# Moving every sixth batch's first one-hots to GpSimd, with another order of first loads, fillings and last items

## The chip, the core and the metric

The kernel runs on one core of a Trainium2 chip. Its engines each follow their own instruction list: TensorE (PE), VectorE (DVE), ScalarE (ACT), GpSimd (POOL) and SyncE (SP, which here only issues transfers). They wait for one another by semaphores. The metric is the device time of one launch in microseconds. Inputs and weights lie in HBM and all arithmetic is in float32, except for some one-hots in bf16.

## The reference, cut to what matters

One decoder layer over 1024 tokens of width 1024, with 16 learned tokens ahead of them. The first half mixes tokens: one projection to four groups of channels with pooling windows and to three gates of a short convolution, norms, and an output projection. The second half picks experts by product keys and sums them:

```python
def peer_retrieve(xn, w_query, sub_keys):
    T = xn.shape[0]
    q = (xn @ w_query).reshape(T, N_PEER_HEADS, 2, D_QUERY_HALF)
    s = jnp.einsum('thpc,hpkc->thpk', q.astype(jnp.float32), sub_keys.astype(jnp.float32))
    s1, i1 = lax.top_k(s[:, :, 0], PEER_TOPK)
    s2, i2 = lax.top_k(s[:, :, 1], PEER_TOPK)
...
    top_s, pos = lax.top_k(cand_s, PEER_TOPK)
    idx = jnp.take_along_axis(cand_i, pos, axis=-1)
    gates = jax.nn.softmax(top_s, axis=-1)
    return idx, gates
...
    def block(args):
        xblk, iblk, gblk = args
        u = expert_u[iblk]
        v = expert_v[iblk]
        act = jax.nn.gelu(jnp.einsum('tkd,td->tk', u, xblk).astype(jnp.float32), approximate=False)
        return jnp.einsum('tk,tkd->td', (gblk * act).astype(v.dtype), v)
```

Here cand_s are the 256 sums of the two halves' best 16, and cand_i their expert ids (i1 * 128 + i2). There are 8 heads, 16384 experts and 16 picked per head, so 128 per token.

The result is added to the residual and normed once more.

## The kernel before

Tokens come in eight tiles of 128, two to a pass, so there are four passes, n = 0 to 3. For four of the tiles the experts are gathered row by row ("rows", 128 experts of u and 128 of v per tile: 1024 rows of 512 KB each, one expert for each of the 128 tokens). For the other four tiles ("dense") all 16384 experts are multiplied with TensorE, and a table of gates, mostly zeros, picks the ones that count.

**The passes (to about 661 us).** TensorE walks through a list `steps`: bcv and pa (input projection), pool, outp, ynorm, outp, turn (transposes), query and score. Four pairs of psum banks are used in turn, so that step s waits until step s - 4 has been emptied, by ACT or by DVE. DVE does the pooling, the convolution and the norms, and between them, at named places, `fill(n, where)`: a planner (`take`) puts units there until their assumed costs (`COST`) reach the number in `FILL`. The units rank the experts of the two tiles of the pass before: four `keys`, `cands`, two `pairs`, `digits`, `pick`, `keep` for each tile, in this order, with the second tile's first keys between the first tile's digits and pick. When nothing is left to rank, a place is filled with rows (`gathered_row`, L1175, 1.35 each by the planner). `pick` needs 16 activations of ACT (`pick_places`, L859, line 864 in the profile), which ACT does right after a step that the planner finds from the costs (`step_at`, `picks_after`). Rows sit in a ring of eight slots: GpSimd issues row r when row r - 8 has been used (L677 to L680).

**The scatter.** The first dense tile's gates are scattered to the table in HBM with 128 indirect transfers of GpSimd, 16 per head (`scatter`, L643). `head_after` (L641) puts heads 0 to 2 behind the issue of row `rows_by[1] + 7` and heads 3 to 7 behind row `rows_by[2] + 7`, where `rows_by[n]` is the number of rows used up to the end of pass n. A head waits for the transfers of the heads before it.

**The gate tables (662 to 821 us).** Three dense tiles' gates become tables by 48 batches of eight tokens. A batch needs two sets of eight one-hots (128x128 each) in one of three buffers. The gated ones are DVE's in all batches (L1467). The first ones are DVE's in even batches (one instruction, L1463) and ACT's in odd ones (eight Square, then one Relu: `first_hots`, L980 to L987, begun one odd batch ahead). TensorE multiplies them (L798), ACT copies the two banks out of psum (L1009), and SyncE stores a chunk each four batches. A buffer comes free when TensorE has done the batch three before. In batches 5, 13, 21, 29, 37 and 45 TensorE also does a score tile of the dense part (L785).

**The dense part (to 2547 us).** TensorE takes tiles of scores (L785, 16 instructions, 6.87 us) and pieces of output sums (L831, the same), eight and eight in groups. ACT makes the gelu (L993), DVE multiplies with the gates (`gate`, L1252) and adds the pieces (`sum`, L1258). Four psum banks hold pieces: piece i waits until sum i - 4 is done. DVE's list is one `order`: the ranking of the last two tiles and all rows that are left (`late`), with gates and sums put between them by their share of the cost, times `DENSE_SPEED`. With a value of 1.0 the last sum comes with the last row. Then follow `total`, `finish` and `dense_out`, and the stores.

**First loads.** SyncE issues the first half of x, the second half, the small vectors, two weight blocks (1 MB each), x of pass 1 and the rest (L521 to L529). ACT squares each half (L876), DVE scales it with g_mix (L1395), TensorE starts with `pa` 0 (L717), one weight block and eight blocks of x.

## Time and profile before

| | us |
|---|---|
| median of 3 runs | 2557.34 |
| lowest, highest | 2557.06, 2560.21 |
| the profiled execution | 2559.86 |
| its span | 2558.1 |

| engine | busy us | share | instructions |
|---|---|---|---|
| PE | 2474.3 | 97% | 7561 |
| DVE | 1971.3 | 77% | 4252 |
| ACT | 424.1 | 17% | 782 |
| POOL | 1452.8 | 57% | 1169 |

The mean granted clock of TensorE is 0.991 of full. The transfers move 857.68 MB, 335 GB/s over the span. The profile is of the profiled execution; its times count from the start of the span. A row of a timeline shows the start, the time taken, the engine, the line of the code, the operation with what it writes and reads, and in brackets how long the engine was idle before it and what ended that. Busy shares are averages over stages with different limits, so each stage is read by itself.

### The profile page before, as it was taken

What the parts mean: (1) busy time and instruction counts of PE and PEld (TensorE: products, weight loads), DVE (VectorE), ACT (ScalarE), POOL (GpSimd) and SP (SyncE); (2) the same over time, 40 slices, a digit from 0 to 9 for tenths busy, and PEclk for the clock granted to TensorE, in tenths of its full rate; (3) what the DMA queues carried; (4) which work ended last, traced back from release to release, by engine and by line L of the source; (5) the groups of instructions that cost most, each with busy time, mean ns of one, the idle gap of its engine ahead of it and who ended that gap; (6) DMA issues with size and microseconds to landing.
All of it is one profiled execution on the core that took longest, in us unless ns stands there. A gap on an engine that the chain in (4) does not pass through costs nothing.

```text
span 2558.1 us, 24120 instructions
## 1 busy us (share of the span) xinstructions
PE 2474.3 (97%) x7561; PEld 1360.4 (53%) x7561; DVE 1971.3 (77%) x4252; ACT 424.1 (17%) x782; POOL 1452.8 (57%) x1169
## 2 busy tenths in 40 slices
PE   8999998998888899999999999999999999999998
PEld 7687785867766344444444444444444444444443
DVE  4308879778779788777898778779787877888877
ACT  0213213221887000110010100000000000000001
POOL 0000487677601267666665767667676776766664
PEclk9999999998999999999999999999999999999999
DMA  8544886865666899989999999999999999999997
GB/s 336 214 156 163 315 300 167 347 188 132 198 190 201 333 356 374 396 318 385 388 413 391 383 385 414 394 418 419 419 386 397 412 394 420 419 407 403 420 401 262
DMA packets 288079, 857.68 MB, mean 335 GB/s; under 512 B 42064, under 2 KB 99408, under 8 KB 273360
## 3 DMA queue, kind: packets, MB, share of 16 engines
q0 software_dynamic: 167184, 541.73, 55.4%
q1 hardware_dynamic: 108416, 289.25, 30.0%
q10 hardware_dynamic: 12352, 25.17, 2.6%
q8 instruction: 60, 0.98, 0.1%
q14 instruction: 67, 0.55, 0.1%
HBM read 807.75 MB, written 48.30 MB: 335 GB/s over the span
## 4 chain that ended last, share of the span: by engine, by line
PE 85%; DVE 6%; ACT 4%; DMA 1%; issue 1%; DVEq 1%; POOL 1%; SPq 1%; ACTq 0%
PE pairs L831 34%; PE pairs L785 33%; PE pairs L699 12%; ACT arena L985 2%; PE pairs L742 1%; PE pairs L717 1%; PE pairs L798 1%; ACT arena L1009 1%; DMA arena<-gate_tables 1%; PE pairs L769 1%; ACT pick_all L864 1%; POOL ring L679 1%; DVE topi L1073 0%; DVE topi L1065 0%; ACT arena L987 0%
## 5 line engine op out<-in xcount | busy, mean ns | idle before, releaser
L679 POOL DMA_INDIRECT ring<-in_expert_u,idx x512 | 660.7, 1290 | 610.7 <-DVE dots L1186 343.5
L831 PE MATMUL pairs<-arena 128*128 128x512 f32 x2048 | 883.4, 593 | 7.0 <-DVE arena L1252 6.3
L785 PE MATMUL pairs<-arena 128*128 128x512 f32 x2048 | 882.5, 592 | 0.0
L679 POOL DMA_INDIRECT ring<-in_expert_v,idx x512 | 574.7, 1122 | 290.2 <-DVE arena L1197 129.9
L1186 DVE CUSTOM_DVE_ANT_0 junk<-ring,xf 128x1024 bf16<-128x1024 f32 x512 | 610.5, 1223 | 157.1 <-DMA ring<-in_expert_u,idx 153.0
L831 PEld LDWEIGHTS pairs<-arena 128*128 128x128 f32 x2048 | 389.6, 190 | 498.4 <-issue 497.5
L785 PEld LDWEIGHTS pairs<-arena 128*128 128x128 f32 x2048 | 388.6, 190 | 486.5 <-issue 486.5
L1197 DVE SCALAR_TENSOR_TENSOR arena<-ring,arena 128x1024 f32<-128x1024 f32 x381 | 471.7, 1284 | 63.8 <-DMA ring<-in_expert_v,idx 62.5
L699 PE MATMUL pairs<-arena 128*128 128x256 f32 (+1 forms) x1792 | 399.7, 386 | 7.2 <-ACT arena L946 4.2
L699 PEld LDWEIGHTS pairs<-arena 128*128 128x128 f32 x1792 | 345.5, 193 | 59.5 <-ACT arena L946 5.1
L993 ACT ACTIVATE arena<-pairs 128x512 f32<-128x512 f32 x128 | 76.4, 597 | 1176.2 <-PE pairs L785 1176.2
L650 POOL DMA_INDIRECT gate_tables<-gate,place x128 | 210.8, 1647 | 57.9 <-issue 38.8
L1197 DVE SCALAR_TENSOR_TENSOR xf<-ring,arena,xf 128x1024 f32<-128x1024 f32 x126 | 154.4, 1282 | 8.8 <-DMA ring<-in_expert_v,idx 8.8
L1252 DVE TENSOR_TENSOR arena<-arena 128x512 f32<-128x512 f32 x128 | 87.6, 688 | 61.2 <-ACT arena L993 48.9
L1258 DVE TENSOR_TENSOR arena<-arena,pairs 128x512 f32<-128x512 f32 x128 | 87.5, 684 | 51.6 <-PE pairs L831 50.9
L1467 DVE TENSOR_SCALAR arena<-iota,arena 128x128 f32<-128x128 f32 x384 | 101.3, 347 | 25.5 <-PE pairs L798 25.5
L742 PE MATMUL pairs<-arena 128*128 128x512 f32 x256 | 114.2, 603 | 5.3 <-DVE arena L1377 5.3
L798 PE MATMUL pairs<-arena 128*128 128x128 f32 x768 | 91.4, 277 | 28.1 <-ACT arena L1009 25.3
L798 PEld LDWEIGHTS pairs<-arena 128*128 128x128 f32 x768 | 88.2, 192 | 34.0 <-issue 30.9
L864 ACT ACTIVATE pick_all<-digit,place 128x256 bf16<-128x256 f32 x128 | 80.4, 723 | 42.0 <-DVE digit L1130 41.7
L742 PEld LDWEIGHTS pairs<-arena 128*128 128x128 f32 x256 | 49.4, 194 | 65.3 <-issue 55.8
L1062 DVE MAX8 tops<-arena 128x8 f32<-128x128 f32 x112 | 24.4, 280 | 61.9 <-ACT arena L961 60.7
(174 smaller groups left out, 1062.1 us busy)
## 6 DMA issues: line engine op xcount, KB each, us to landing
arena<-in_w_all SPq DMA_DIRECT2D x80, 1024.0 KB, 6.1
arena<-in_uT SPq DMA_DIRECT2D x128, 512.0 KB, 6.7
arena<-in_expert_v SPq DMA_DIRECT2D x128, 512.0 KB, 8.8
arena<-gate_tables SPq DMA_DIRECT2D x32, 1024.0 KB, 11.3
gate_tables<-arena SPq DMA_DIRECT2D x11, 2048.0 KB, 9.0
gate_tables<-junk ACTq DMA_DIRECT2D x4, 2048.0 KB, 14.0
ring<-in_expert_u,idx POOLq DMA_INDIRECT x512, 8.9
ring<-in_expert_v,idx POOLq DMA_INDIRECT x512, 8.3
```

The lines of the kernel that those rows point to most:

```text
L650: nc.gpsimd.indirect_dma_start(out=g_flat, out_offset=bass.IndirectOffsetOnAxis(ap=place[:, k:k + 1], axis=0), in_=gate[:, k:k + 1], in_of ...
L679: nc.gpsimd.indirect_dma_start(out=ring[:, r % RING, :], out_offset=None, in_=expert_u if table == "u" else expert_v, in_offset=bass.Indir ...
L699: last = nc.tensor.matmul(out_, w[:, k, c * P:(c + 1) * P], xn[:, k, :], start=(k == 0), stop=(k == KD - 1))
L742: last = nc.tensor.matmul(pair[:, q * 512:(q + 1) * 512], yT[:, NG * (1 - half) + k, t * P:(t + 1) * P], w_out[q].rearrange("p k n -> p (k ...
L785: last = nc.tensor.matmul(score_bank[x], uslot[:, x % USLOTS, k * P:(k + 1) * P], xfT[:, k, :], start=(k == 0), stop=(k == KD - 1))
L798: last = nc.tensor.matmul(g_bank[(2 * b + m) % 4][:, q * KEYS:(q + 1) * KEYS], hots[:, c, 0, 4 * m + q, :], hots[:, c, 1, 4 * m + q, :], s ...
L831: last = nc.tensor.matmul(o_bank[n % 4], gated[:, x % GSLOTS, t * P:(t + 1) * P], vrows[:, j, half * 512:(half + 1) * 512], start=(j == 0) ...
L864: last = nc.scalar.activation(pick_hot[:, a], digit[:].rearrange("p h s k -> p k (h s)"), ACT.Square, scale=32.0, bias=place16[:, a:a + 1])
L1186: nc.vector.tensor_tensor_reduce(out=junk[:, r % 2, :], in0=row, in1=xf[:, t % 2, :], scale=1.0, scalar=0.0, op0=ALU.mult, op1=ALU.add, ac ...
L1197: nc.vector.scalar_tensor_tensor(out=to[:, k % 2, :], in0=row, scalar=weight[:, k:k + 1], in1=h2 if k == 0 else to[:, k % 2, :], op0=ALU.m ...
L1252: nc.vector.tensor_tensor(s, s, gtab[a // GJ % 2][:, :, a % GJ, :], ALU.mult).then_inc(w_ready, 1)
L1467: last = nc.vector.tensor_scalar(hots[:, c, 1, t, :], iota[:], routeT[:, 1, k:k + 1], routeT[:, 2, k:k + 1], ALU.is_equal, ALU.mult)
```

## The change

Batches with b % 6 = 5 (5, 11, ..., 47) get their first one-hots from GpSimd instead of ACT: eight `tensor_scalar` with is_equal per batch, behind the point at which GpSimd has issued row `rows + RING - 1`, where `rows` is the number of rows used ahead of the tables. The semaphore of the first one-hots is split in two. The smalls are loaded first, and a weight block is issued after each half of x. The numbers of `FILL` for outp, query, y and y2 get smaller, and `DENSE_SPEED` becomes 0.99.

```diff
@@ -76,9 +76,9 @@
 FILL = [[(f"conv{g}", 4.0) for g in range(4)] + [("gate", gate), ("y", y), ("y2", y2), ("outp", outp), ("query", query)]
-        for gate, y, y2, outp, query in ((0.0, 0.0, 0.0, 0.0, 0.0), (4.0, 13.0, 6.0, 10.0, 70.0), (4.0, 13.0, 6.0, 10.0, 70.0), (0.0, 10.0, 3.0, 0.0, 66.0))]
+        for gate, y, y2, outp, query in ((0.0, 0.0, 0.0, 0.0, 0.0), (4.0, 13.0, 6.0, 2.0, 66.0), (4.0, 13.0, 6.0, 2.0, 66.0), (0.0, 8.0, 0.0, 0.0, 66.0))]
 HOT_FILL = 0.0
-DENSE_SPEED = 1.0
+DENSE_SPEED = 0.99
 FIRST_FILL = 42.0
 KEYS_ROWS = 3
@@ -295,7 +295,8 @@
         d_gates = sem("d_gates")
         turned = sem("turned")
         turned_out = sem("turned_out")
-        hot_first = sem("hot_first")
+        hot_act = sem("hot_act")
+        hot_pool = sem("hot_pool")
         hot_gated = sem("hot_gated")
         table_full = sem("table_full")
         table_out = sem("table_out")
@@ -496,6 +497,11 @@
             elif kind == "sum" and a == GROUPS - 1 and b % 2 == 1:
                 beside[x].append(("dense_root", b // 2))
+
+
+        BY_POOL = [b for b in range(BATCHES) if b % 6 == 5]
+        BY_ACT = [b for b in range(BATCHES) if b % 2 == 1 and b % 6 != 5]
+
         block = ctx.enter_context(nc.Block())
         @block.sync
@@ -518,11 +524,11 @@
                     sp.wait_ge(pe_step if by == "step" else w_freed, count)
                 sp.dma_start(wslot[k % WSLOTS].rearrange("p k n -> p (k n)"), w_all[uses[k][0], :, :]).then_inc(w_loaded[k % WSLOTS], 16)
+
+            sp.dma_start(smalls[:], small).then_inc(small_in, 16)
             for s in range(2):
                 sp.dma_start(xnT[0][:, s * NG:(s + 1) * NG, :], hT[:, s * NG:(s + 1) * NG, BASE[0]:BASE[0] + COLS]).then_inc(x_first[s], 16)
-            sp.dma_start(smalls[:], small).then_inc(small_in, 16)
-            load_w()
-            load_w()
+                load_w()
             load_x(1)
             sp.dma_start(poolw.rearrange("p g n -> p (g n)"), pool_w).then_inc(const_in, 16)
             sp.dma_start(skT, sub_keys).then_inc(const_in, 16)
@@ -657,6 +663,16 @@
                     pool.wait_ge(rows_used, first_row["u", t - 2] + HK)
                 pool.dma_start(xf[:, t % 2, :], of_tile(xf_d, GATHERED_TILE[t])).then_inc(xf_in[t % 2], 16)
+            def first_hots(b):
+                c = b % HOTBUFS
+                pool.wait_ge(table_full, 2 * (b - HOTBUFS) + 2)
+                if b // (P // HOTS) > 0:
+                    pool.wait_ge(turned_out, b // (P // HOTS))
+                for t in range(HOTS):
+                    k = b * HOTS + t
+                    last = nc.gpsimd.tensor_scalar(hots[:, c, 0, t, :], iota[:], routeT[:, 0, k:k + 1], None, ALU.is_equal)
+                last.then_inc(hot_pool, 1)
+
             for i, (table, t) in enumerate(ROWS):
                 if table == "u":
                     load_xf(t)
@@ -674,6 +690,10 @@
                     pool.dma_start(h2, of_tile(h2_d, GATHERED_TILE[t])).then_inc(h2_in, 16)
                 for k in range(HK):
                     r = HK * i + k
+                    if r == rows + RING:
+
+                        for b in BY_POOL:
+                            first_hots(b)
                     if r >= RING:
                         pool.wait_ge(rows_used, r - RING + 1)
                     nc.gpsimd.indirect_dma_start(out=ring[:, r % RING, :], out_offset=None, in_=expert_u if table == "u" else expert_v,
@@ -789,8 +809,10 @@
             for b in range(BATCHES):
                 c = b % HOTBUFS
                 pe.wait_ge(hot_gated, b + 1)
-                if b % 2 == 1:
-                    pe.wait_ge(hot_first, b // 2 + 1)
+                if b in BY_ACT:
+                    pe.wait_ge(hot_act, BY_ACT.index(b) + 1)
+                elif b in BY_POOL:
+                    pe.wait_ge(hot_pool, BY_POOL.index(b) + 1)
                 for m in range(2):
                     if 2 * b + m >= 4:
                         pe.wait_ge(table_out, 2 * b + m - 3)
@@ -984,7 +1006,7 @@
                 for t in range(HOTS):
                     nc.scalar.activation(hots[:, c, 0, t, :], iota[:], ACT.Square, scale=-1.0, bias=routeT[:, 0, b * HOTS + t:b * HOTS + t + 1])
                 act.drain()
-                nc.scalar.activation(hots[:, c, 0], hots[:, c, 0], ACT.Relu, scale=-4.0, bias=ones[:, 0:1]).then_inc(hot_first, 1)
+                nc.scalar.activation(hots[:, c, 0], hots[:, c, 0], ACT.Relu, scale=-4.0, bias=ones[:, 0:1]).then_inc(hot_act, 1)
             def gelu_tile(x):
                 if x >= GSLOTS:
@@ -998,7 +1020,7 @@
             for b in range(BATCHES):
                 if b - 1 in AFTER_BATCH:
                     gelu_tile(AFTER_BATCH.index(b - 1))
-                if b % 2 == 1 and b + 2 < BATCHES:
+                if b % 2 == 1 and b + 2 in BY_ACT:
                     first_hots(b + 2)
                 for m in range(2):
                     n = 2 * b + m
```

With the new numbers the planner puts into the places (units of the tile ranks, with the rows used):

| place | before | after |
|---|---|---|
| pass 1, outp | pick 0, keep 0, keys 1 (third) | pick 0 |
| pass 1, query | from the fourth keys of 1; rows 0 to 27 | keep 0, third and fourth keys of 1, ...; rows 0 to 18 |
| pass 2, outp | pick 2, keep 2, keys 3 (third) | pick 2 |
| pass 2, query | ...; rows 28 to 56 | keep 2, third keys of 3, ...; rows 19 to 39 |
| pass 3, y2 | digits 4 | nothing |
| pass 3, query | keys 5, ...; rows 57 to 63 | digits 4, keys 5, ...; rows 40 to 46 |
| ACT's picks for ranks 1 and 3 | after query step 0 | after query step 1 |
| ACT's picks for rank 4 | after the second outp | after the second turn |

In the dense part the order has gate 127 behind row 991 before and behind row 1001 after the change. Its last items were sum 4, rows 1012 to 1015, sum 5, dense_out 1, rows 1016 to 1019, sum 6, rows 1020 to 1023, sum 7, dense_out 2, dense_out 3, total 3, finish 3; they become sum 4, rows 1022 and 1023, total 3, sum 5, dense_out 1, sum 6, sum 7, dense_out 2, dense_out 3, finish 3.

## Rows read from the trace of the kernel before

**Rows 1.** The chain that ended last, by time: start us, us, what.

```profile
817.47 3.59 PE pairs L798 x32
```

**Rows 2.** The page's 40 slices: what the transfers moved.

```profile
GB/s 336 214 156 163 315 300 167 347 188 132 198 190 201 333 356 374 396 318 385 388 413 391 383 385 414 394 418 419 419 386 397 412 394 420 419 407 403 420 401 262
```

**Rows 3.** Timeline of the start: start us, us, engine, line, operation [idle before].

```profile
6.28 1.11 ACT L876 ACTIVATE arena<-arena 128x1088 f32<-128x1088 f32 x1 [0.42 <-DMA arena<-in_hT]
...
9.04 5.62 PE L717 MATMUL pairs<-arena 128*128 128x272 f32 x16 [9.04 <-DMA arena<-in_w_all]
```

**Rows 4.** Timeline of TensorE, passes 1 to 3.

```profile
271.40 3.44 PE L748 MATMUL pairs<-ident,arena 128*128 128x128 f32 x16 [2.23 <-DVE arena L1387]
...
437.30 1.07 PE L748 MATMUL pairs<-ident,arena 128*128 128x128 f32 x8 [3.24 <-DVE arena L1387]
...
565.44 7.03 PE L742 MATMUL pairs<-arena 128*128 128x512 f32 x16
...
577.53 9.61 PE L742 MATMUL pairs<-arena 128*128 128x512 f32 x16 [5.07 <-DVE arena L1377]
```

**Rows 5.** Query stretches: busy us (instructions) by engine, granted clock, DMA share, GB/s.

```profile
118.00:175.00 57.00, 55.49 (x256) 48.56 (x256) 1.64 (x4) 4.45 (x5) 0.72 (x1) 1.00 0.46 161
276.00:335.00 59.00, 58.54 (x256) 50.69 (x256) 48.96 (x155) 15.07 (x22) 31.35 (x19) 0.95 0.89 330
441.00:499.00 58.00, 57.45 (x256) 50.13 (x256) 46.25 (x149) 13.68 (x20) 38.73 (x26) 0.96 0.84 311
```

**Rows 6.** Timeline of GpSimd: scatters of heads, then row loads.

```profile
513.00 1.62 POOL L650 DMA_INDIRECT gate_tables<-gate,place  x1 [0.30 <-issue]
...
679.12 1.56 POOL L650 DMA_INDIRECT gate_tables<-gate,place  x1 [0.30 <-issue]
...
688.56 0.94 POOL L679 DMA_INDIRECT ring<-in_expert_u,idx  x1 [0.30 <-issue]
```

**Rows 7.** Timeline of DVE: a pick, and where two fillings end.

```profile
304.19 2.29 DVE L1136 TENSOR_TENSOR pick_all<-topf,pick_all 128x4096 bf16<-128x4096 bf16 x1 [3.65 <-ACT pick_all L864]
...
345.57 0.44 DVE L1302 TENSOR_TENSOR arena<-arena 128x271 f32<-128x271 f32 x1
...
510.40 0.44 DVE L1302 TENSOR_TENSOR arena<-arena 128x271 f32<-128x271 f32 x1
```

**Rows 8.** Timeline of GpSimd: a select, row loads beside DVE and alone.

```profile
1.15 0.29 POOL L631 TENSOR_SCALAR_AFFINE_SELECT ident<-ident 128x128 f32<-128x128 f32 x1 [0.63 <-DVE ident L1048]
...
299.37 1.99 POOL L679 DMA_INDIRECT ring<-in_expert_u,idx  x1 [0.30 <-issue]
301.66 0.94 POOL L679 DMA_INDIRECT ring<-in_expert_u,idx  x1 [0.30 <-issue]
```

**Rows 9.** Timeline of the table stage: batch 5, a plain pair.

```profile
676.35 2.02 PE L798 MATMUL pairs<-arena 128*128 128x128 f32 x16 [1.01 <-ACT arena L1009]
...
693.02 2.44 ACT L985 ACTIVATE arena<-iota,arena 128x128 f32<-128x128 f32 x8
...
694.35 1.22 DVE L1463 TENSOR_TENSOR arena<-iota,arena 128x1024 f32<-128x1024 f32 x1
...
695.49 4.20 DVE L1467 TENSOR_SCALAR arena<-iota,arena 128x128 f32<-128x128 f32 x16
...
698.50 2.44 ACT L985 ACTIVATE arena<-iota,arena 128x128 f32<-128x128 f32 x8
```

**Rows 10.** DVE by line, 2000 to 2200: busy us, mean ns, idle before.

```profile
L1186 DVE CUSTOM_DVE_ANT_0 junk<-ring,xf 128x1024 bf16<-128x1024 f32 x66 | 79.1, 1224 | 23.9 <-DMA ring<-in_expert_u,idx 23.6
L1197 DVE SCALAR_TENSOR_TENSOR arena<-ring,arena 128x1024 f32<-128x1024 f32 x51 | 63.7, 1285 | 15.2 <-DMA ring<-in_expert_v,idx 14.8 <-issue 0.2
```

**Rows 11.** Waits of DVE, 816 to 2547: us in total, times, longest.

```profile
DVE arena L1258 <- PE pairs L831: 50.9, 42, 1.6
DVE arena L1252 <- ACT arena L993: 48.9, 30, 3.6
```

**Rows 12.** Timeline of the end.

```profile
2550.74 1.22 DVE L1238 TENSOR_TENSOR xf<-xf 128x1024 f32<-128x1024 f32 x1
```

## Prediction

> **What bounds the kernel now.** I read the page first (busy shares, the 40 slices, the granted clock), then the chain of work in order of time, the stretches between its changes of character, and for each stretch what its leading engine waited for. The reader should see three parts. Up to about 661 us the projections run in four passes (n = 0 to 3). From 662 to 821 us come the gate tables, 48 batches of one-hots, whose last TensorE work starts at 817.47 [rows 1]. After a loading gap of some 38 us the dense part runs from 859 us on without a break to 2547 us. In the dense part only order and supply matter: TensorE's tiles and pieces of 6.87 us each follow one another, and the change takes none of them away. So time can be won ahead of 821 us and behind 2547 us, and lost anywhere.
>
> The sum is made against the profiled execution: 2559.86 us, of which the span is 2558.1. It is 2.5 us above the median of the runs, 2557.34, and I take differences from it over to the median.
>
> **First loads.** TensorE starts at 9.04, held by the first weight block, which is queued behind both halves of x and the small vectors [rows 3]. In the new order one half of x (544 KB) is no longer ahead of it: at the 336 GB/s of the page's first slice [rows 2] that is 1.6 us. The second half of x now lands about when the weights do today, just ahead of 9.04 (I take 8.8) instead of 6.2; its square takes 1.1 us [rows 3] and the first scaling 0.3, which make it ready at 10.2. TensorE, started at 7.4, reaches its fifth block (0.70 us each, 5.62 for eight) at 10.2. So there is hardly a second wait, and I take 1.3 us (0 to 2).
>
> **Fillings.** The planner's lists can be followed. In passes 1 and 2 "outp" keeps only pick; keep and one keys unit go to the head of "query", and the rows there fall from 28 to 19 and from 29 to 21. In pass 3 digits leaves "y2" for "query". So 47 rows instead of 64 are used before the tables, and 17 more remain. Removed from TensorE's path:
> - pass 1: idle 2.23 ahead of the turns, which then took 3.44 at a lowered clock [rows 4], and a query stretch of 58.54 us of matmuls at a mean granted clock of 0.95 of full, where pass 0 took 55.49 at 1.00 [rows 5]. The clock had fallen to its lower level (1.2 of 2.4 GHz) after the idle time. With DVE's add_half some 6.5 us earlier the turns don't wait: 2.2 + 3.0 and about 0.8 of the turns, 6.0.
> - pass 2: 3.24 idle ahead of the turns [rows 4] and 0.4 between them, 57.45 against 55.49 in the query [rows 5], some 1.3 of slow turns: 7.0. A short wait at ynorm stays, because DVE gains about as much as TensorE.
> - pass 3: 5.07 idle and an output product of 9.61 instead of 7.03 [rows 4]: 7.7. ACT's pick for rank 4, 10 us long, stood between two outp steps and kept the y root waiting; it moves behind the turns.
>
> Together with the start the tables could begin 22.0 us earlier.
>
> **What GpSimd does meanwhile.** Here the two halves of the change meet. first_hots for batch 5 stands in GpSimd's order behind five heads of scatter and seven row loads. Today the scatters start at 513.00, the last one at 679.12, and the seventh row load ends at 689.5 [rows 6]: 176.5 us of issue work that nothing here shortens. They start when DVE has used the last row of pass 2's filling, 510.4 [rows 7]. How much earlier is that? In pass 1 the picks on ACT now follow the second query step, not the first: they end at 311.8 (TensorE's query begins at 272.9 and a step takes 13.9; ACT needs 11.1 behind the second) instead of 304.2 [rows 7], and the 9 rows fewer behind them are worth 15.6 at 1.73 us a row, the 34 us of 311.5 to 345.6 over 20 rows, so DVE leaves the pass 8 us earlier than 345.6 [rows 7]. In pass 2 the same placing ends the picks 2 us later than today and there are 8 rows fewer (13.9): 11.9 earlier. With the start that is 13.2. GpSimd thus comes to batch 5 at 689.5 - 13.2 = 676.3. One set is eight operations on 128x128. No row shows this operation on GpSimd. Nearest below is its select on 128x128, 0.29 us; nearest above its indirect issue, 0.94 us alone and up to 1.99 beside DVE's row work [rows 8]. I take 0.35, as the select has the same shape, so 3 us a set (2.3 to 8). TensorE could have begun batch 5 at 676.35 - 22.0 = 654.3 [rows 9] and begins it at 679.3. It waits 25 us there, so that batch 5 begins 3 us later than today: all that the start and the fillings won, and 3 us more, is paid back in this one wait.
>
> **The tables.** From batch 5 to the end takes 144.7 us today (676.35 to 821.06) [rows 1, 9]. An odd batch's first one-hots and four copies make ACT's pair of batches 5.48 long (693.02 to 698.50) [rows 9]. DVE's pair is 1.14 + 4.20 = 5.3 [rows 9], TensorE's 3.6 [rows 1], and once in eight batches a score tile adds 6.87. Taking a third of the sets from ACT therefore uncovers DVE at once, 0.2 us lower in a plain pair; more of the gain lies in the pair with the score tile. TensorE alone would need 43 x 1.8 + 6 x 6.87 = 119 and DVE alone 43 x 2.67 = 115; I take 138, nearer to today's 144.7 because DVE's 5.3 follows ACT's 5.48 so closely (range 126 to 150). The tables end at 679.3 + 138 = 817.3, 3.7 us earlier than today.
>
> A set on GpSimd reads and writes SBUF beside DVE. The issue of a row load took 1.99 us while DVE worked on rows with two inputs and 0.94 while it waited [rows 8], so the two do hold each other up in some pairings. The Trainium skill ("SBUF — State Buffer", section "SBUF: two separate sides") says that GpSimd and a DVE instruction of two SBUF inputs, or of a two-port mode, exclude each other for whole instructions. If it holds for the one-hots, the tables end at 834 instead of 817; no row here shows the two side by side, and the case is a rival below.
>
> **The dense part.** It has DENSE_SPEED 0.99 and 17 rows more. Counted in the two orders, 928 rows stand ahead of gate 127 today, 955 after the change: 27 more. Between 2000 and 2200 us DVE waited for rows alone and used 66 + 51 of them, 1.71 us a row with the items between [rows 10], so 27 rows cost 46 us. DVE's idle time for TensorE and ACT in 816 to 2547 is 50.9 + 48.9 = 99.8 us [rows 11]; this is the cover, and about 54 are left of it. It isn't even: at 2000 to 2200 there is none, and psum lets a sum be three pieces (20 us) late, a last gate of a group only the two tiles behind it, and gate 127 nothing. I take 4 us of TensorE waiting at the last group (0 to 20).
>
> **The end.** Today total 3 starts at 2550.74, behind the dense outputs, then come root and finish [rows 12]. In the new order total and root lie ahead of the last three sums, and after dense_out 3 only finish is left: the 1.2 of total and 1.6 of waiting for the root fall away, 2.9 us (2 to 3).
>
> Sum: -3.7 + 4 - 2.9 = -2.6, so 2557.34 - 2.6 = 2554.7 us.
>
> **Rivals.**
> 1. GpSimd comes earlier. If the rows of the passes land faster than 1.7 us each or the picks on ACT aren't late, DVE's end of pass 2 follows TensorE's 20 us instead of 13, and with a table pace of 130 the sum is -2.6 - 7 - 7 = 2541. For it: DVE's waits in both passes are for rows alone. Against it: the picks follow TensorE's steps. Chance 0.27.
> 2. Slower, by the supply of rows in the dense part. The 54 us of cover are an average, and where DVE is bound by rows the new order asks for 2.6% more of them a step. If rows come at 1.71 us throughout, also near the end, gate 127 is late by 10 to 20 us, as each row too few ahead of it costs 1.7 us. This decides from the point where 27 more rows use up the cover between 2200 and 2490. For it: no cover at all in 2000 to 2200 [rows 10]. Against it: much of the 99.8 lies behind 2200. Time 2554.7 - 4 + 17 = 2568. Chance 0.20.
> 3. DVE and GpSimd exclude each other in the tables. Seven sets of 2.4 us taken from DVE, which is then the bound, are 17 us, and the tables end at 834 instead of 817: 2571. For it: 1.99 beside 0.94 [rows 8]. Against it: a set is short beside six batches. The Trainium skill's sentence above would give this result. Chance 0.10.
> 4. The change doesn't do what it says: ACT's sets weren't the pace, and the passes gain nothing since another wait follows each that goes. Then only start and end are left, 2553 to 2558. Chance 0.05.
>
> The forecast has 0.38. It lies between 2549 and 2561.
>
> **How the numbers follow.** A measurement of this kernel can tell about 0.2% from no change, 5 us. Faster by more than that (under 2552.2): all of rival 1, 0.09 of the forecast: 0.36. Slower (over 2562.5): rivals 2 and 3, less a little of 2: 0.29. The rest is 0.35. The range takes in rivals 1 and 2 and reaches to the price of 3: 2538 to 2573. The forecast's own range is 2549 to 2561.
>
> **What would show it.** In the profile after: the first TensorE matmul near 7.4; no idle ahead of the turns in passes 1 and 2; the query stretches of these passes at a clock of 1.00; the first batch of the tables near 640; a wait of TensorE of some 25 us ahead of batch 5, released by GpSimd; the first GpSimd set near 676 and eight operations of about 0.35 us; the end of the tables near 817; DVE's idle time for TensorE and ACT near 50 us; a wait of a few us at the last group's first piece; 8 us between the last matmul and the end instead of 11. The prediction is wrong if GpSimd reaches batch 5 before TensorE does, if its operations take over 0.7 us each (a set must fit in two batches), or if DVE's cover in the dense part goes to nothing.

## The result

The changed kernel is slower: 2575.7 us, median of five runs (2567.2 to 2578.0), beside 2560.1 for five runs of the kernel before. The ratio is 1.0052, with a 95% interval of 1.0038 to 1.0066. In ten later runs it was 1.0020 (1.0000 to 1.0041), beside a kernel before that ran in 2555 to 2578. The two medians stand for a loss of some 5 to 13 us, and the two intervals together reach from nothing to 17. The forecast was 2554.7 with a range up to 2573; the median of 2575.7 lies above that range.

The profiled execution took 2578.0 us, with a span of 2576.2, against 2558.1 before: 18.1 longer. The table sets the steps of the sum beside each other. The "waits" of TensorE in the dense part are summed here from the starts of successive instructions of tiles and pieces: what lies between two starts beyond the 0.43 us of one, wherever that is over 0.12 us. They hold the idle time and the slower instructions at a lowered clock behind it. "Early" are those within 25 us of the first piece.

| profiled execution, us | before | after, predicted | after, measured |
|---|---|---|---|
| first TensorE matmul | 9.04 | 7.4 | 8.82 |
| tables begin | 662.0 | 640 | 644.0 |
| batch 5 begins | 676.3 | 679.3 | 678.1 |
| tables end | 821.0 | 817.3 | 819.3 |
| waits around the first pieces | 9.0 | 9 | 12.3 |
| waits in the rest of the dense part | 0 | 4 | 18.7 |
| last matmul ends | 2546.8 | 2547 | 2567.8 |
| from there to the end of the span | 11.3 | 8 | 8.3 |

So the first third ended close to where the sum had it: what the passes won went into one wait at batch 5. The 18 us come from behind 821 us: -1.8 from the tables, +3.3 and +18.7 of waits, +0.8 of single instructions behind them that start 0.1 us or less too late, and -3.0 at the end.

**The profile after, beside the rows of before.** Timeline of TensorE, to be held against [rows 3] and [rows 4] (start us, us, engine, line, operation, idle before it and what ended it; the lines of the code stand some 20 further on in the changed kernel):

```profile
8.82 5.35 PE L737 MATMUL pairs<-arena 128*128 128x272 f32 x16 [8.82 <-DMA arena<-in_w_all]
...
269.03 1.91 PE L768 MATMUL pairs<-ident,arena 128*128 128x128 f32 x16
...
347.45 8.84 PE L719 MATMUL pairs<-arena 128*128 128x256 f32 x27 [4.25 <-DMA arena<-in_w_all]
...
429.56 1.91 PE L768 MATMUL pairs<-ident,arena 128*128 128x128 f32 x16
...
573.57 1.06 PE L768 MATMUL pairs<-ident,arena 128*128 128x128 f32 x8 [3.79 <-DVE arena L1409]
...
655.34 1.95 PE L820 MATMUL pairs<-arena 128*128 128x128 f32 x16
678.07 3.75 PE L820 MATMUL pairs<-arena 128*128 128x128 f32 x16 [20.78 <-issue]
681.62 8.30 PE L805 MATMUL pairs<-arena 128*128 128x512 f32 x16
```

The turns of passes 1 and 2 no longer wait, and take 1.91 us, where those of pass 1 took 3.44. Two waits are left in the passes, and both stood there before:

```profile
351.96 8.22 PE L699 MATMUL pairs<-arena 128*128 128x256 f32 x37 [1.92 <-DMA arena<-in_w_all]
...
591.78 1.06 PE L748 MATMUL pairs<-ident,arena 128*128 128x128 f32 x8 [3.77 <-DVE arena L1387]
...
678.21 7.03 PE L785 MATMUL pairs<-arena 128*128 128x512 f32 x16
```

The wait for a weight block grew from 1.92 to 4.25 us, as TensorE comes to it earlier; the one for DVE between the turns of pass 3 stayed (3.77, now 3.79). At 678.07 is the wait at batch 5. Its end is put down to "issue"; the timeline of GpSimd shows who it was:

```profile
501.85 1.61 POOL L656 DMA_INDIRECT gate_tables<-gate,place  x1 [0.30 <-issue]
...
672.32 0.94 POOL L699 DMA_INDIRECT ring<-in_expert_u,idx  x1 [0.31 <-issue]
673.30 4.67 POOL L673 TENSOR_SCALAR arena<-iota,arena 128x128 f32<-128x128 f32 x8
695.37 6.23 POOL L673 TENSOR_SCALAR arena<-iota,arena 128x128 f32<-128x128 f32 x8 [17.40 <-PE pairs L820]
```

The scatters start at 501.85 instead of 513.00 [rows 6], GpSimd gets through them and seven row loads, makes the first set in 4.67 us, and TensorE starts the moment it ends. The windows show what else the wait costs (columns as in [rows 5]):

```profile
273.00:331.00 58.00, 56.80 (x273) 49.94 (x272) 44.45 (x162) 15.56 (x22) 24.11 (x18) 1.00 0.84 323
...
433.00:489.00 56.00, 55.49 (x256) 48.56 (x256) 42.84 (x161) 13.31 (x21) 19.86 (x14) 1.00 0.84 298
```

```profile
678.00:682.00 4.00, 3.93 (x17) 3.92 (x18) 0.14 (x1) 0.73 (x2) 0.00 (x0) 0.50 0.01 5
682.00:690.00 8.00, 8.00 (x19) 3.39 (x18) 3.14 (x9) 1.79 (x3) 0.00 (x0) 0.86 0.00 0
```

The query stretches of passes 1 and 2 now run at a granted clock of 1.00, where [rows 5] had 0.95 and 0.96. Behind the long wait the granted clock is 0.50, the lower of the two levels: batch 5 and the tile behind it take 3.75 + 8.30 us, against 2.02 [rows 9] + 7.03 before. So the long wait costs another 3 us behind it.

And the waits of TensorE from 862 us on. Before, this view has no line at all:

```profile
PE pairs L853 <- DVE arena L1274: 10.9, 6, 4.3
PE pairs L853 <- DVE arena L1280: 2.9, 3, 1.6
```

These are pieces of output that wait for DVE's gates (L1274) and sums (L1280). The view counts 13.8 us of idle time, and that is all there is. The starts give 18.7, as they also hold what the lowered clock costs behind a wait: behind the 4.32 us of idle time at 2516.86 the next matmuls start 0.85 us apart instead of 0.43 (granted clock 0.56 from 2517 to 2521), and behind the 2.59 at 1198.17 as well (0.63 from 1200 to 1204), some 2 us each. The other seven waits, of 1.6 us or less, have no such matmuls behind them. The early waits of 12.3 us are 9.1 of idle time and 3.2 of this. DVE's own rows tell why the gates are late, in the waits of 816 to 2560 us; the lines for PE and ACT belong against [rows 11]:

```profile
DVE junk L1208 <- DMA ring<-in_expert_u,idx: 165.6, 156, 4.3
DVE arena L1219 <- DMA ring<-in_expert_v,idx: 94.6, 99, 2.1
DVE xf L1219 <- DMA ring<-in_expert_v,idx: 24.6, 29, 2.3
...
DVE arena L1280 <- PE pairs L853: 6.5, 5, 2.5
...
DVE arena L1274 <- ACT arena L1015: 2.8, 3, 2.3
```

DVE now waits 285 us for rows (205 before) and 9 us for TensorE and ACT (99.8 before). The 27 rows more used up 90 of the 100 us of cover, not the 46 that the prediction gave them. Yet DVE gets through no more rows: 116 between 2000 and 2200 us by the two lines of [rows 10], where the kernel before had 117. The chain of work that ended last shows such a case (start us, us, what): a row that is under way for 10.7 us, rows and a gate of DVE back to back behind it, and then the gate that the piece at 2516.86 had waited 4.3 us for.

```profile
2498.65 10.72 DMA ring<-in_expert_v,idx
...
2511.22 1.33 DVE xf L1219 x2
...
2516.03 0.69 DVE arena L1274
2516.72 0.14 issue
2516.86 51.00 PE pairs L853 x114
```

### The profile page after: what moved, and what is told of

Its sections match the earlier page's. It is cut to its first block, busy times and chain, and to the rows that moved or that the text cites. A ratio compares the mean times of both kernels' runs of the same rounds, so it can differ in the third digit from the quotient of the medians.

```text
span 2576.2 us, 24110 instructions
## 1 busy us (share of the span) xinstructions
PE 2476.7 (96%) x7561; PEld 1361.5 (53%) x7561; DVE 1976.7 (77%) x4252; ACT 399.8 (16%) x710; POOL 1495.8 (58%) x1233
## 4 chain that ended last, share of the span: by engine, by line
PE 50%; DMA 19%; POOL 14%; issue 8%; DVE 5%; ACT 2%; SPq 1%; DVEq 0%; ACTq 0%
PE pairs L719 15%; POOL ring L699 14%; PE pairs L853 14%; DMA ring<-in_expert_u,idx 11%; PE pairs L805 10%; DMA ring<-in_expert_v,idx 6%; PE pairs L762 4%; PE pairs L820 2%; PE pairs L737 2%; DVE junk L1208 1%; DVE arena L1219 1%; DMA arena<-gate_tables 1%; PE pairs L789 1%; DVE arena L1489 1%; DMA arena<-in_w_all 1%
## 5 line engine op out<-in xcount | busy, mean ns | idle before, releaser
L699 POOL DMA_INDIRECT ring<-in_expert_u,idx x512 | 649.6, 1269 | 517.3 <-DVE dots L1208 246.8
L699 POOL DMA_INDIRECT ring<-in_expert_v,idx x512 | 588.0, 1148 | 258.2 <-issue 121.6
L1489 DVE TENSOR_SCALAR arena<-iota,arena 128x128 f32<-128x128 f32 x384 | 105.3, 353 | 18.3 <-PE pairs L820 18.3
L1280 DVE TENSOR_TENSOR arena<-arena,pairs 128x512 f32<-128x512 f32 x128 | 87.0, 680 | 17.9 <-PE pairs L853 17.5
L673 POOL TENSOR_SCALAR arena<-iota,arena 128x128 f32<-128x128 f32 x64 | 45.2, 724 | 92.8 <-PE pairs L820 92.7
L1274 DVE TENSOR_TENSOR arena<-arena 128x512 f32<-128x512 f32 x128 | 87.2, 685 | 14.8 <-DMA arena<-gate_tables 11.3
```

Of the source, the lines that this page charges most:

```text
L699: nc.gpsimd.indirect_dma_start(out=ring[:, r % RING, :], out_offset=None, in_=expert_u if table == "u" else expert_v, in_offset=bass.Indir ...
L1274: nc.vector.tensor_tensor(s, s, gtab[a // GJ % 2][:, :, a % GJ, :], ALU.mult).then_inc(w_ready, 1)
L1280: nc.vector.tensor_tensor(piece, piece, o_bank[b % 4], ALU.add).then_inc(o_added, 1)
L1489: last = nc.vector.tensor_scalar(hots[:, c, 1, t, :], iota[:], routeT[:, 1, k:k + 1], routeT[:, 2, k:k + 1], ALU.is_equal, ALU.mult)
```

## The experiments

The first four take the change apart and the next two take parts back; the others ask who limits the rows, and whether the two prices found can be paid in another way. Each ratio is to the kernel before on the same chip, with its 95% interval. Where it says "one run", there is a profile and a single time. The waits are those of one profiled execution each; for the changed kernel, for speed 1.0 in it and for the fillings alone that is the slowest of their runs, so that their waits may be a few us over the usual.

### One part at a time

**The dense order alone.** In the kernel before:

```diff
-DENSE_SPEED = 1.0
+DENSE_SPEED = 0.99
```

> The kernel before with DENSE_SPEED 0.99 alone. Theory 1 (supply): TensorE stalls in the dense part when the rows that must be used ahead of a gate or a sum come too slowly, and what counts is the sum of the 17 rows more and the 1% more. Here only about 10 more rows stand ahead of gate 127, 17 us of DVE's 100 us of idle time: 0 to 4 us of stalls in the dense part, and an end 2.7 us shorter, so -3 to +2 us against before. Theory 2 (the order of the last items costs it by itself, because DVE is late for gate 127): a stall of 5 to 9 us at the last group already here, and +3 to +7 us.

Measured: 2560.9 us, ratio 0.9995 (0.9978 to 1.0011). Dense waits 0.1 us, early ones 10.1; the end takes 8.3 us instead of 11.3. Ten more rows ahead of gate 127 cost TensorE nothing, and the gain at the end is there but too small to be told in the median.

**The fillings alone.** In the kernel before, the changed `FILL` and nothing else.

> The kernel before with the changed fillings alone: 47 rows ahead of the tables instead of 64. The tables begin 18 us earlier, as in the changed kernel, and nothing waits for GpSimd, so they end some 17 us earlier. Theory 1 (supply): 17 more rows are 29 us of supply, which the 100 us of idle time of DVE cover nearly: 0 to 6 us of stalls; in sum -17 to -9 us against before. Theory 3 (each row put behind the tables costs TensorE time, as the dense part was at the limit of supply already): 17 x 1.3 = 22 us of stalls, in sum about +5.

Measured: 2551.5 us, ratio 0.9947 (0.9930 to 0.9965). The tables begin at 642.2 and, with no wait at batch 5, end at 803.9: 17.2 us earlier than before. But dense waits of 12.1 us and early ones of 10.8 (9.0 before) appear, and in this execution, of 2556.9 us, the last matmul comes only 2.9 earlier; in the ratio 13.6 us are left. Seventeen rows more behind the tables are enough to make TensorE wait.

**GpSimd's one-hots alone.** In the kernel before, `BY_POOL`, `BY_ACT`, the two semaphores and `first_hots` of GpSimd.

> The kernel before with the one-hots on GpSimd alone (b % 6 = 5), loads, fillings and speed as before. GpSimd ends its row loads at 689.5 as before and its first set takes 4.7 us beside nothing, so batch 5 begins at 694.2 instead of 676.35: 18 us of wait. The other 43 batches took 141 us in the changed kernel against 144.7. Theory 1: the tables end 14 us later and the dense part is as before: +12 to +16 us. Rival: the wait is absorbed by a faster table stage, 0 to +5.

Measured: 2573.7 us, ratio 1.0028 (1.0009 to 1.0047). Batch 5 begins at 693.5 instead of 676.3, held by GpSimd's set, and the tables end 11.3 us later, at 832.3; the last matmul follows 12.9 later. This part alone is a loss. TensorE and GpSimd meet there in the same way as in the changed kernel:

```profile
676.33 1.95 PE L821 MATMUL pairs<-arena 128*128 128x128 f32 x16
693.49 3.75 PE L821 MATMUL pairs<-arena 128*128 128x128 f32 x16 [15.21 <-issue]
```

**First loads alone.**

```diff
+            sp.dma_start(smalls[:], small).then_inc(small_in, 16)
             for s in range(2):
                 sp.dma_start(xnT[0][:, s * NG:(s + 1) * NG, :], ...)
-            sp.dma_start(smalls[:], small).then_inc(small_in, 16)
-            load_w()
-            load_w()
+                load_w()
```

> The changed order of first loads alone. The step of the prediction gave it 1.3 us. The changed kernel's profile showed a first matmul at 8.82 instead of 9.04 and nothing left of it in the first pass, so now: the first matmul near 8.8, the end of pass 0 and the start of the tables within 1 us of the kernel before, and the span within 0.2% of it.

Measured, one run: 2559.7 us, span 2557.9, the first matmul at 9.18, the tables from 662.0 to 821.0: no gain over the one profile of the kernel before. The first matmul varies from execution to execution, though. In the seven profiles with the old order of loads, of kernels that differ elsewhere, it starts at 9.04 to 9.91 (mean 9.60), in the seven with the new one at 8.33 to 9.18 (mean 8.90). So the step brings some 0.7 us at the first matmul; in the median of the runs this can't be seen. In the changed kernel the first half of x, alone in front now, is squared at 5.99 instead of 4.75 and the second at 10.04 instead of 6.28 [rows 3], while the weight block lands at 8.8. That fits transfers that share the bandwidth while they are under way, although they are issued one behind the other: with 544 KB less in front of it the weight block gains less than half of the 1.6 us of those bytes. That they share it is argued, not shown.

### The changed kernel with one part taken back

**Speed 1.0 in the changed kernel.**

```diff
-DENSE_SPEED = 0.99
+DENSE_SPEED = 1.0
```

> The changed kernel with DENSE_SPEED 1.0 again. Theory 1 (supply): 10 rows fewer ahead of gate 127, so the stalls of the dense part fall from 22 to 5 to 12 us and the end is 2.7 us longer again: -7 to -14 us against the changed kernel, about 2565 us. Theory 2 (the order of the last items): only the stall at the last group (7 us) goes. Theory 3 (17 rows): stalls stay at 18 to 22, and the time is that of the changed kernel or 2 us above it.

Measured: 2567.4 us, ratio 1.0009 (0.9991 to 1.0027). Dense waits fall from 18.7 to 9.2, and the end grows back to 11.3. The same ten rows that cost nothing in the kernel before cost 9.5 us here.

**Batch 5 back on ACT.** GpSimd makes the sets of 11, 17, ..., 47.

```diff
-        BY_POOL = [b for b in range(BATCHES) if b % 6 == 5]
-        BY_ACT = [b for b in range(BATCHES) if b % 2 == 1 and b % 6 != 5]
+        BY_POOL = [b for b in range(BATCHES) if b % 6 == 5 and b > 5]
+        BY_ACT = [b for b in range(BATCHES) if b % 2 == 1 and b not in BY_POOL]
```

> The changed kernel with batch 5's first one-hots on ACT again; GpSimd keeps batches 11, 17, ..., 47. Theory 1: GpSimd's order behind the scatters costs the tables 20.8 us at batch 5. Without it batch 5 runs at about 657 and batch 11, which begins at about 678 then, finds its set just in time (GpSimd comes free at 673). The tables end 14 to 20 us earlier, near 802; the dense part keeps its stalls of 20 us: 14 to 20 us under the changed kernel, 2556 to 2562. Rival: ACT, DVE and TensorE had used the wait to run ahead, so only 5 us come back.

Measured: 2555.6 us, ratio 0.9976 (0.9963 to 0.9989). Batch 5 begins at 660.0 and the tables end at 802.3, 17.0 earlier than in the changed kernel; dense waits stay, 17.3. From batch 5 to the end it is 142.3 us, where the fillings alone, without GpSimd, take 147.4. So the seven sets that are left do speed up the tables by some 5 us, but the set of batch 5 costs 17 through its wait, and the dense loss has nothing to do with the sets.

### Who limits the rows

Two theories were left for the late gates. Rows may be limited by what the transfers carry per us, or by latency: GpSimd's issue and eight slots of the ring.

**Ring of seven.** In the kernel before, `RING = 7`.

> The kernel before with a ring of 7 row slots instead of 8. If rows are limited by the latency of a slot's round trip (issue, landing, use, next issue), the supply becomes 7/8 as fast, a row takes 1.94 us instead of 1.7, and the dense part becomes 150 to 220 us longer. If it is limited by what the transfers move in all (397 GB/s in 900 to 2500 us), the ring is deep enough and the time grows by 0 to 25 us.

Measured, one run: 2576.9 us, span 2575.2, dense waits 14.4. A slot fewer costs some 16 us; a supply held by latency alone would lose an eighth of its pace, ten times as much. That it costs anything may be because the ring evens out the transfers' pace; this is argued, not shown.

**Rows of half the length.** The changed kernel, in which a row's load brings only 512 of the 1024 numbers (the other half of the ring stays zero; that part of the experts is left out of the computation), with as many transfers, issues and slots.

> The changed kernel with rows of half the length: each row transfer brings only the first 512 of 1024 numbers, the other half of each ring slot is zero from the start, so part of the computation is left out. DVE does the same work per row. If the limit is the number of bytes, DVE's waits for rows (285 us) fall to under 60 us and the stalls of TensorE in the dense part go to the 9 us at its beginning: about 2555 us. If it is the issue on GpSimd or the latency of the round trip, the waits stay above 180 us and so do the stalls.

Measured, one run: 2544.8 us, no dense wait, early ones 2.7. That is 10 us under what was expected, in good part because the early waits went too. The windows, first the changed kernel, then this one:

```profile
1500.00:2000.00 500.00, 499.01 (x1163) 220.55 (x1162) 397.34 (x531) 25.60 (x42) 351.89 (x291) 1.00 1.01 404
2000.00:2500.00 500.00, 495.88 (x1155) 219.01 (x1154) 414.28 (x459) 26.31 (x43) 356.44 (x304) 1.00 1.02 412
```

```profile
1500.00:2000.00 500.00, 500.00 (x1166) 221.35 (x1165) 405.00 (x550) 24.02 (x39) 386.34 (x303) 1.00 0.75 251
2000.00:2500.00 500.00, 500.00 (x1166) 221.35 (x1165) 411.61 (x436) 29.74 (x48) 364.91 (x305) 1.00 0.77 257
```

The last two columns are the share of time in which the transfer engines are busy, and GB/s. With whole rows the share is 1.0, with half rows 0.76, at the same number of rows. DVE's waits for rows fall from 285 to 91 us, and those for TensorE and ACT rise to 154 (44 of them put down to issue stand beside these). The transfers were the limit. Fewer bytes a row may also shorten the way of each row; that this alone isn't it, the ring of seven shows. The kernel before has the same in its own windows, and this is the view the prediction did not read:

```profile
1500.00:2000.00 500.00, 500.00 (x1167) 221.37 (x1166) 401.21 (x536) 25.22 (x41) 350.48 (x294) 1.00 1.01 404
2000.00:2500.00 500.00, 500.00 (x1167) 221.37 (x1166) 405.84 (x443) 27.01 (x44) 342.44 (x298) 1.00 1.01 409
```

One can work it out: a step of 6.87 us of TensorE needs 512 KB of weights, 76 GB/s, and a row of 512 KB each 1.71 us [rows 10] is 307 GB/s; together 383, with the gate tables the 404 to 409 of these rows. So 1.71 us a row is no pace of DVE or GpSimd but what the transfers leave over. The Trainium skill ("Perfetto Trace Analysis", section "Roofline") puts the ceiling of a core's 16 transfer engines at about 435 GB/s; the highest slice of the page after has 420.

### Paying for the rows in another place

**Twenty rows inside the tables.** The fillings alone, and five rows behind each of batches 16, 24, 32 and 40, where the transfers have room (238 to 301 GB/s at a share of 0.80 to 0.97 in windows from 640 to 803 us of the next kernel, even with these rows in it).

```diff
-HOT_FILL = 0.0
+HOT_FILL = 6.7
...
-            plan["hots", b] = take(HOT_FILL) if b % 3 == 2 else []
+            plan["hots", b] = take(HOT_FILL) if b % 8 == 0 and b > 8 else []
```

> The changed fillings alone (as e2_fill), with 20 of the rows taken into the table stage: five each behind the batches 16, 24, 32 and 40, where DVE stood idle for 4.8 to 5.4 us. 67 rows are used ahead of the dense part instead of 47. Theory 1 (supply): the tables end within 3 us of those of e2_fill, the dense stalls return to the 9 us at its beginning: about -20 us against before, 6 to 12 us under e2_fill. Rival: the rows aren't landed in time or delay ACT's and TensorE's batches, the tables get 8 to 15 us longer, and nothing is won over e2_fill.

Measured: 2542.4 us, ratio 0.9937 (0.9917 to 0.9957), dense waits 0, the tables end at 799.9. Twenty rows of DVE inside the tables cost them nothing, and the whole gain of the fillings is kept: the span is 2540.5, 17.6 less than before.

**The same with speed 0.99.**

```diff
-DENSE_SPEED = 1.0
+DENSE_SPEED = 0.99
```

> The fillings alone, 20 rows used inside the tables, and the dense order of speed 0.99. If the order of 0.99 costs only by asking for more rows ahead of gate 127 (27 with the 17 of the fillings), the 20 rows used early pay it: dense waits of TensorE under 3 us, the tail 8.5 instead of 11.4, and 2 to 3 us less than the same kernel with speed 1.0 (ratio 0.9937 there): 0.9925. If the 0.99 order is bad in itself (late gates at a group's end whatever the stock), dense waits of 8 to 10 us as between speed 1.0 and 0.99 in the changed kernel, and a ratio of 0.996 or more.

Measured: 2542.3 us, ratio 0.9930 (0.9905 to 0.9954), dense waits 0.2, the end 8.3 us. The order of 0.99 is not bad in itself: with rows in stock it asks for nothing that TensorE has to wait for. Its 3.0 us at the end show in the profile but not in the median, which equals that of the same kernel with speed 1.0.

**All parts, with both prices taken out.** The changed kernel with GpSimd's sets from batch 11 on, each where it is due between the row loads, and the twenty rows inside the tables.

```diff
-                    if r == rows + RING:
-                        for b in BY_POOL:
-                            first_hots(b)
+                    for b in {0: (11, 17), 5: (23,), 10: (29,), 15: (35, 41), 20: (47,)}.get(r - rows_by[-1] - RING, ()):
+                        first_hots(b)
```

> The changed kernel (order of first loads, fillings, speed 0.99, GpSimd's one-hots) with two differences: GpSimd makes the sets of batches 11 to 47 only, each in its queue between the row loads where it is due, and 20 rows are used inside the tables. If nothing but the wait at batch 5 and the supply of rows in the dense part made the change slow, both are gone: tables from about 643 to 797, dense waits under 3 us, span near 2536, ratio 0.991 to 0.993. If a third cost hangs on GpSimd's sets (shared SBUF access with VectorE, row loads late behind the sets), the tables end after 801 or the dense waits stay over 8 us, and the ratio is 0.995 or more.

Measured: 2549.0 us, ratio 0.9945 (0.9925 to 0.9965). The dense waits are gone, but the tables end at 808.9, 6.4 us later than without GpSimd's sets. Its waits of TensorE in the tables:

```profile
PE pairs L818 <- ACT arena L1029: 9.2, 7, 1.6
PE pairs L818 <- DVE arena L1487: 8.7, 4, 3.2
PE pairs L818 <- issue: 8.2, 3, 4.6
```

In the kernel without the sets (speed 0.99) there are 26.5 us for ACT's copies and none of the other two. The sets relieve ACT, but TensorE waits for a set (issue) and for DVE's gated one-hots instead, and the granted clock is 0.89 to 0.96 in four of five windows, where it is 1.00 without them. A set takes 6.3 us here (56 operations, 788 ns each). The expectation of 797 was wrong: a third cost hangs on the sets, and beside rows in the tables they no longer pay. How much of it is the sets' own length, their place in GpSimd's queue or the clock isn't separated.

**The changed kernel again**, on the chip of the last three.

> The changed kernel once more, beside the others of this call on the same chip. If its 12 us over the kernel before are a property of the order, it comes out 0.3 to 0.7% slower than before here too, with dense waits of TensorE for VectorE's gates of 10 to 20 us in the profiled execution. If they were a matter of that chip or that hour, the ratio is within 0.2% of 1.

Measured: 2570.6 us, ratio 1.0020 (1.0000 to 1.0041), batch 5 at 674.4, the tables end at 813.3, dense waits 21.4. The lost time stands in the same places. The kernel before came out at 2564.1 here (2555 to 2578 in 20 runs). Its slower runs may have dense waits of their own; only one of its runs has a profile, so this is open.

### The dense waits against the rows

Rows ahead of gate 127, counted against the kernel before, and the dense waits of the profiled executions:

| kernel | rows more | dense waits, us |
|---|---|---|
| twenty rows inside the tables | -2 | 0 |
| before; GpSimd's sets alone | 0 | 0; 0 |
| twenty rows inside, speed 0.99; all parts, both prices out | +7 | 0.2; 0 |
| speed 0.99 alone | +10 | 0.1 |
| fillings alone; changed with speed 1.0 | +17 | 12.1; 9.2 |
| changed, twice; changed with batch 5 on ACT | +27 | 18.7, 21.4; 17.3 |

Up to 10 rows cost nothing, 17 cost about 10 us and 27 about 19: 1.0 to 1.7 us for each row above ten. No run lies between 10 and 17. Half-length rows at +27 cost 0.

## Why the prediction was wrong

**First loads (-1.3 predicted; -0.2 in these two profiles, -0.7 over all).** The step took the weights to wait in a queue behind all bytes of x. The order moved the landing of x more than theirs; -0.7 lies inside the step's own bounds of 0 to 2.

**Fillings (-22.0 with the start, measured -18.0).** Each pass did what was said or more: by the starts of TensorE's rows pass 1 won 6.8 us up to its scores (6.0 predicted, and the start's 1.3), pass 2 8.7 (7.0) and pass 3 7.8 (7.7). Turns at 269.03 and 429.56 have no idle ahead of them, and the query runs at a clock of 1.00. Left out was the weight block that TensorE already waited for at 351.96: it now comes to it earlier, waits 2.3 us longer, and the low clock behind that costs 2.8 more, so 5.1 us are lost there. Another 0.2 goes in the last query stretch.

**GpSimd's arrival at batch 5 (batch 5 at 679.3, measured 678.1).** The path is the one described, but three errors cancel in the number. The scatters start 11.2 us earlier (13.2 predicted). They and the row loads take 171.4 us, not the 176.5 that "nothing here shortens": the heads wait 13.6 us for one another's transfers instead of 19.2. So GpSimd is there at 673.3 instead of 676.3. And a set takes 4.7 us instead of 3, inside the bounds of 2.3 to 8: 0.58 us for one operation on 128x128, not 0.35 (0.72 in the mean of all 64, over the 0.7 that the prediction gave as a sign of being wrong). That they meet within 1.2 us is luck. The wait of 20.8 us (25 predicted) ate the fillings' gain as described, and the run without this set shows it by 17.0 us at the end of the tables. Rival 1, GpSimd coming earlier, fell.

**The tables from batch 5 on (138, measured 141.2).** The term left out the clock: 3 us of the 141.2 are the low clock behind the long wait. The sets themselves give 5 us, as the 142.3 and 147.4 of the two kernels without that wait show.

**Rival 3, DVE and GpSimd exclude each other (2571).** It has a time near the measured one, and is still not what happened: the tables ended at 819, not 834. DVE's sixteen one-hots beside the set at 695.37 took 5.10 us, and the next ones without a set beside them 4.18:

```profile
694.94 5.10 DVE L1489 TENSOR_SCALAR arena<-iota,arena 128x128 f32<-128x128 f32 x16
...
706.36 4.18 DVE L1489 TENSOR_SCALAR arena<-iota,arena 128x128 f32<-128x128 f32 x16
```

The sets of 11 and 17 took 6.23 and 5.61 us, the one at 673.30, with DVE idle, 4.67. Where the difference comes from, the single operations show. The last of the set at 695.37 meets DVE's first one-hots (L1485), an instruction with two inputs:

```profile
698.02 0.66 POOL L673 TENSOR_SCALAR arena<-iota,arena 128x128 f32<-128x128 f32 x1
...
699.92 1.21 DVE L1485 TENSOR_TENSOR arena<-iota,arena 128x1024 f32<-128x1024 f32 x1
699.94 1.66 POOL L673 TENSOR_SCALAR arena<-iota,arena 128x128 f32<-128x128 f32 x1
```

In the changed kernel seven of the 64 operations meet such an instruction and take 1.46 to 1.66 us, against 0.59 alone, while DVE's instruction keeps its 1.21. Beside the gated one-hots (one tensor input, L1489) the two work at the same time, and the 41 operations that meet nothing else take 0.60 to 0.74. The Trainium skill ("SBUF — State Buffer", section "SBUF: two separate sides") would have GpSimd and a DVE instruction of two inputs exclude each other for a whole instruction, and for the two-input one-hots the trace agrees. So there is an exclusion, but it falls once on each set and on GpSimd, some 1 us a time, not on DVE, which is the engine that rival 3 had pay for it.

**The dense part (+4, measured +22): the step that failed.** The rows were counted rightly (27) and priced at the pace that the rows show (46 us). Wrong was the cover. DVE's 99.8 us of idle for TensorE and ACT [rows 11] was taken for time in which more rows could be used. It isn't, because the transfers don't rest while DVE does: in the kernel before their share is 0.94 to 0.96 from 900 to 1200 us and 0.99 or more from there to 2500. In such a pause they fill the ring, and DVE finds its next rows ready; a row more asked for earlier finds no transfer that could have brought it earlier, and the pause is turned into a wait for rows. Hence 80 us more of waits for rows, 90 fewer for TensorE and ACT, and a real slack of about 10 rows, 17 us, where 99.8 us at 1.71 would be 58 rows. It is also what the prediction had named as a sign of being wrong, that DVE's cover goes to nothing (9 us are left). Rival 2 named this mechanism, and gave it 2568 at a chance of 0.20. It put the loss at the last group; 7.6 us of the 18.7 fell there and the rest from 1113 to 2195 us. It had the price of each row too many at 1.7 us, against 1.0 to 1.7 measured. What hid its weight was that its condition (27 rows against the cover) was tried with the same wrong cover.

**The end (-2.9, measured -3.0).** Right.

In the sum: the last matmul came 21.0 us later than before. That is 22.0 of waits in the dense part and 0.8 of single instructions behind them, less the 1.8 that the tables gave back, where 3.7 were expected. Both halves of the change are in the result: the first set on GpSimd cost the 17 us that the fillings had won, and the 17 rows of the fillings then cost the dense part 9 to 12 us and the ten of the new order another 9.5, because they have to be brought in a stretch where the transfers are full.

## What to carry to other kernels

Before an engine's idle time is booked as cover, ask which resource fills its queue and whether that one rests too: here the view of waits showed 100 us of cover, and the column of the transfers' share, 1.0, showed that there was almost none. Work taken out of an early stage comes back in the stage that is full; put it where both engine and transfers have room, as the twenty rows inside the tables, with which the fillings are worth 0.6%. And an operation given to an idle engine must be placed by when that engine's queue gets there: one set of 4.7 us behind 170 us of queued transfers cost 17.

## What the hardware showed

- A compare of 128x128 float32 on GpSimd takes 0.58 us with DVE idle (4.67 for 8) and 0.72 in the mean of 64, against DVE's 0.26 for the same shape (4.18 for 16). It runs beside DVE's one-input compares, and is held for as long as an instruction of DVE with two inputs lasts (1.46 to 1.66 us against 0.59).
- After a wait of 20.8 us the granted clock is 0.50 for the 4 us that follow and 0.86 in the next 8; after one of 4.25 us it is 0.57 for 7 us. Either costs about 3 us on top of the wait, and waits of 2.6 and 4.3 us in the dense part cost some 2 more each. Behind those of 1.6 us or less in the dense part nothing was lost but 0.1 us.
- The transfers of this kernel saturate at 404 to 412 GB/s over 500 us, with a share of 1.0, of which three quarters are indirect rows (307 of 404).
- Taking 544 KB from in front of the first weight block brought it in 0.7 us earlier in the mean of seven profiles each (8.90 against 9.60 us), not the 1.6 us of those bytes.
